# A mix stage rebuilt: entering states in their own slots, scans moved into the stage before, tiles backward, two buffers, a written-out pipeline

## What is computed

```
def step(S, blk):                      # one chunk of a scan
    ...
    o = A @ v + (q * exp(b)) @ S       # inside the chunk, and from the entering state S
    S = exp(b_end) * S + (k * exp(b_end - b)).T @ v
...
x = x + g1 * (concat[y_hg, y_ssd, y_ret] @ w_out)
h = rms_norm(x) * (1 + sc2) + sh2      # and then the router and the experts
```

## Time and profile before

| | us |
|---|---|
| three timed runs, median (lowest to highest) | 3216.76 (3212.91 to 3219.59) |
| the profiled execution, its own time | 3213.58 |
| span of the profiled execution | 3211.7 |
| mix stage of layer 0, barrier 3 to barrier 4 | 786.8 to 1094.1 |
| mix stage of layer 1 | 2349.5 to 2654.6 |
| PE busy, share of the span | 84% |
| DVE, POOL and ACT busy | 41%, 22% and 20% |

### The profile page before, as it was taken

One profiled execution on the slowest core, in us unless ns is written; L12 is line 12 of the kernel. 1 busy time (PEld: TensorE's weight loads), 2 busy tenths in 40 slices (PEclk: granted clock), 3 DMA queues, 4 the chain that ended last, 5 costly groups with the idle time before them and its releaser, 6 DMA issues.

```text
span 3211.7 us, 43754 instructions
## 1 busy us (share of the span) xinstructions
PE 2698.0 (84%) x16228; PEld 1980.1 (62%) x16228; DVE 1322.8 (41%) x2786; ACT 643.3 (20%) x1363; POOL 692.4 (22%) x782
## 2 busy tenths in 40 slices
PE   2899889998489569999769997999938982999992
PEld 0455566664255269999725555666525542999992
DVE  1355535555555432222105554455654545222221
ACT  0333312222011012211113332222211110122211
POOL 0000023443433112222100000444453320212211
PEclk9999989999688779999979998999968885999996
DMA  7432231112333447777373332211133324887763
GB/s 271 165 111 94 91 116 68 68 61 86 115 122 120 177 136 277 276 276 279 109 277 113 100 119 97 73 68 72 59 122 113 126 86 172 280 277 275 278 202 132
DMA packets 221546, 486.30 MB, mean 151 GB/s; under 512 B 26446, under 2 KB 82462, under 8 KB 218910
## 3 DMA queue, kind: packets, MB, share of 16 engines
q1 hardware_dynamic: 210046, 442.17, 38.3%
q0 software_dynamic: 11264, 37.76, 4.6%
q10 hardware_dynamic: 112, 4.72, 0.4%
HBM read 400.96 MB, written 88.36 MB: 152 GB/s over the span
## 4 chain that ended last, share of the span: by engine, by line
PE 73%; DVE 10%; DMA 5%; ACT 3%; issue 3%; POOL 2%; SPq 2%; POOLq 1%; DVEq 0%; ACTq 0%
PE bank L749 21%; PE bank L782 16%; PE bank L793 8%; PE bank L756 6%; DVE work L1404 6%; PE bank L720 5%; PE bank L839 4%; ACT work L1123 3%; PE bank L931 3%; DMA work<-gates_d 2%; PE bank L869 2%; PE bank L818 1%; DMA work<-x_d 1%; POOL small L1877 1%; PE bank L1047 1%
## 5 line engine op out<-in xcount | busy, mean ns | idle before, releaser
L749 PE MATMUL bank<-work 128*128 128x512 f32 (+1 forms) x1728 | 728.9, 569 | 13.3 <-ACT work L1123 8.7
L1123 ACT ACTIVATE work<-bank 128x256 f32<-128x256 f32 (+7 forms) x782 | 301.3, 419 | 1195.7 <-PE bank L782 256.9
L749 PEld LDWEIGHTS bank<-work 128*128 128x128 f32 x1728 | 316.3, 191 | 326.4 <-issue 287.2
L782 PE MATMUL bank<-work 128*128 128x144 f32 x4096 | 512.5, 288 | 2.2 <-DVE work L1404 2.2
L782 PEld LDWEIGHTS bank<-work 128*128 128x128 f32 x4096 | 508.8, 192 | 3.0 <-issue 2.4
L720 PE MATMUL bank<-cst,work 128*128 128x128 f32 (+3 forms) x1920 | 258.5, 284 | 217.1 <-DVE work L1839 87.9
L1404 DVE TENSOR_TENSOR work<-work 128x256 f32<-128x256 f32 (+3 forms) x629 | 356.3, 595 | 182.9 <-PE bank L931 98.7
L720 PEld LDWEIGHTS bank<-cst,work 128*128 128x128 f32 (+3 forms) x1920 | 220.8, 145 | 273.2 <-DVE work L1839 88.8
L1123 ACT ACTIVATE work<-work 128x256 f32<-128x256 f32 (+3 forms) x247 | 169.0, 685 | 980.0 <-DVE work L1404 376.3
L1404 DVE TENSOR_TENSOR work<-bank,work 128x144 f32<-128x144 f32 (+2 forms) x218 | 91.3, 421 | 544.4 <-ACT work L1123 503.3
L839 PE MATMUL bank<-work 128*128 128x512 f32 x576 | 273.2, 631 | 17.0 <-ACT work L1123 17.0
(11 more groups left out here) (155 smaller groups left out, 2343.8 us busy)
## 6 DMA issues: line engine op xcount, KB each, us to landing
work<-in_w_gate_dram SPq DMA_DIRECT2D x32, 2048.0 KB
work<-in_w_up_dram SPq DMA_DIRECT2D x32, 2048.0 KB
work<-in_w_down_dram SPq DMA_DIRECT2D x32, 2048.0 KB
work<-in_w_ada_dram SPq DMA_DIRECT2D x32, 1024.0 KB, 6.3
work<-x_d SPq DMA_DIRECT2D x45, 512.0 KB, 4.0
work<-sum_d SPq DMA_DIRECT2D x18, 1024.0 KB, 5.0
work<-in_w_ada_dram SPq DMA_DIRECT2D x4, 4096.0 KB, 19.2
work<-in_w_in_dram SPq DMA_DIRECT2D x8, 2048.0 KB, 19.6
```

The costliest lines, as they stand in the source:

```text
L749: mm = pe.matmul(bank[:, bk, 0:w.shape[-1]], h[:, ch, :], w[:, ch, :], start=(ch == 0), stop=(ch == DC - 1))
L782: mm = pe.matmul(bank[:, 4 + f, o:o + CAP_S + CAP_P], w[:, ch, f * P:(f + 1) * P], e_xt[:, ch, :], start=(ch == 0), stop=(ch == DC - 1))
L1123: return act.activation(out, in_, func, **kw)
```

## The change

Six things change, in all three stages of a layer that lie before the top-k choice.

1. **Slots.** The context's additions to the forward state go to slot 9 (`slot_f(0) = NT`), so the latents' entering states can be loaded at the start of the local stage (`load_states`) and the context's final states be stored inside it (`store_states`, behind tile 2). Tile 0 of the mix stage no longer multiplies with its zero states.
2. **Scans.** The forward scan is spread over the tiles of the local stage on POOL (`step_on`, one step behind `weighted_values` of tiles 2 to 8). The backward scan is done on POOL in the mix stage, two steps in the prologue and one per tile (`step_back`). The copies of `entering` are gone: `inter` reads the slots.
3. **Order.** The mix stage takes the tiles as 0, 8, 7, ..., 1 (`MIX`).
4. **Buffers.** `r_o`, `r_qe` and `r_g` have two sets; they, the gains, `w_out` and `r_x` lie over the weights of the stages before. ACT issues the load of `w_out` behind the last but one tile of the local stage, and SP the loads of tile 0 and of the gains there.
5. **Pipeline.** `mix` is split into `mix_states` and `mix_gate`, the loops are written out, and `inter` runs two tiles ahead of `project`; in a round PE does `turn_y(j)`, `inter(j + 2)`, `project(j, 0)`, `turn_xn(j - 1)`, `project(j, 1)`, `router(j - 1)`.
6. **State matmuls.** L967, L1038 and L1055 are split by head or group: twice the instructions, half the columns of weights and of moving data, each half written to its own 64 partitions. The copies out of the banks take 128 partitions at a time, half as many.

```diff
+        MIX = (0,) + tuple(range(NT - 1, 0, -1))
...
+        def slot_f(t):
+
+            return NT if t == 0 else (t + 1) % NT
...
+            def load_mix(l, j):
+                t, p = MIX[j], j % 2
+                if j >= 2:
+                    sp.wait_ge(sem["r_y"], by("r_y", l * NT + j - 1))
+                    sp.sem_inc(tick, 1)
+                name, _ = set_of(l, j)
+                sp.dma_start(r_o2[p], o_d[tile_rows(t), :]).then_inc(sem[name], 16)
+                sp.dma_start(r_g2[p], gates_d[tile_rows(t), :]).then_inc(sem[name], 16)
+                sp.dma_start(r_qe2[p].rearrange("p a b -> p (a b)"), qe_d[t]).then_inc(sem[name], 16)
...
                 load_sums(0, l * NT + 1)
+                load_states(l)
                 store_gates(0, l * NT + 1)
...
+                    if t == 2:
+                        store_states(l, l * NT + 1)
                     if t + 1 < NT:
                         store_gates(t + 1, n + 1)
+                    if t + 2 == NT:
+                        sp.wait_ge(sem["z_mm"], by("z_mm", n + 1))
+                        sp.sem_inc(tick, 1)
+                        load_mix(l, 0)
+                        load_res(0, l * NT + 1)
+                        for dst, src, m in ((gain_row[:, 0:256], hg_norm_g[l], 256), (gain_row[:, 256:768], ssd_norm_g[l], 512),
+                                            (gain_row[:, 768:1024], ret_norm_g[l], 256)):
+                            sp.dma_start(dst, row_bc(src, m)).then_inc(sem["gain_in"], 16)
                 for name in ("z_st", "l_st"):
                     sp.wait_ge(sem[name], by(name, l * NT + NT))
                     sp.sem_inc(tick, 1)
                 barrier(sp, l, 3)
...
+                load_mix(l, 1)
+                load_mix(l, 2)
+                load_mix(l, 3)
+                for j in range(1, NT):
+                    n = l * NT + j + 1
+                    load_res(MIX[j], n)
+                    store_sum(MIX[j - 1], n - 1)
+                    if j + 3 < NT:
+                        load_mix(l, j + 3)
+                    store_normed(MIX[j - 1], n - 1)
...
                     for i in range(4):
-                        mm = pe.matmul(bank[:, 2, i * P:(i + 1) * P], l_rkb[:, i * P:(i + 1) * P], l_rv[:, (i % 2) * P:(i % 2 + 1) * P], start=True, stop=True)
+                        for half in range(2):
+                            mm = pe.matmul(bank[rows(half), 2, i * HD:(i + 1) * HD], l_rkb[:, i * P + half * HD:][:, :HD], l_rv[:, (i % 2) * P + half * HD:][:, :HD],
+                                           start=True, stop=True)
...
                     for d in range(2):
-                        pe.matmul(bank[:, 6 + d, :], l_tm[:, 4, :], l_v2[:, d, :], start=True, stop=True).then_inc(sem["l_dS"], 1)
+                        for g in range(2):
+                            mm = pe.matmul(bank[rows(g), 6 + d, 0:256], l_tm[:, 4, g * HD:(g + 1) * HD], l_v2[:, d, g * 256:(g + 1) * 256], start=True, stop=True)
+                        mm.then_inc(sem["l_dS"], 1)
...
+                inter(l, 1)
+                pe.wait_ge(sem["a_rowcp"], by("a_rowcp", nl))
+                turn_y(l * NT + 1)
+                inter(l, 2)
                 pe.wait_ge(sem["r_w_in"], by("r_w_in", nl))
...
+                for j in range(1, NT):
+                    n = l * NT + j + 1
                     turn_y(n)
+                    if j + 2 < NT:
+                        if j >= 2:
+                            pe.wait_ge(sem["r_lgc"], by("r_lgc", n - 2))
+                        inter(l, j + 2)
                     project(n, 0)
                     turn_xn(n - 1)
                     project(n, 1)
...
+                    if t + 2 == NT:
+                        act.dma_start(r_w, w_out[l].rearrange("(c p) n -> p c n", p=P)).then_inc(sem["r_w_in"], 16)
...
-                for g in range(2):
-                    src = bank[rows(g), 2, :].rearrange("p (d q v) -> p d q v", d=2, q=2)[:, :, :, 64 * g:64 * g + 64]
-                    ev(st_f[rows(g), t + 1, RB[0]:RB[0] + 2, :], src[:, 0])
-                    last = ev(st_b[rows(g), t, RB[1]:RB[1] + 2, :], src[:, 1])
+                src = bank[:, 2, 0:256].rearrange("p (d q v) -> p d q v", d=2, q=2)
+                ev(st_f[:, slot_f(t), RB[0]:RB[0] + 2, :], src[:, 0])
+                last = ev(st_b[:, t, RB[1]:RB[1] + 2, :], src[:, 1])
...
-                ln = Link(dve, "s_fs", nl)
-                for tile in range(1, NT - 1):
-                    step_f = r_y[:, 0:512].rearrange("p (a b) -> p a b", b=HD)
-                    ln(tt(step_f, st_f[:, tile], bc(dec[:, tile, 0, :], HD)))
-                    ln(tt(st_f[:, tile + 1], st_f[:, tile + 1], step_f, ALU.add), last=(tile == NT - 2))
...
+                mix_gate(l, 0)
                 diagonal(0, nl)
                 diagonal(1, nl)
...
+                normed(l, 0)
+                spread(24, 8, scale2, shift2)
+                for j in range(1, 3):
+                    mix_states(l, j)
+                    mix_gate(l, j)
+                    sums(l * NT + j + 1)
+                    if j == 1:
+                        normed(l, 1)
...
+                for j in range(1, NT):
+                    n = l * NT + j + 1
+                    gated(0 if j == 1 else 1, n - 1)
+                    if j + 1 < NT:
+                        normed(l, j + 1)
+                    if j + 2 < NT:
+                        mix_states(l, j + 2)
                     second_norm(n - 1)
+                    if j + 2 < NT:
+                        mix_gate(l, j + 2)
+                    modulated(MIX[j - 1], n - 1)
+                    if j + 2 < NT:
+                        sums(n + 2)
+                    logits(MIX[j - 1], n - 1)
...
+            def step_back(l, t):
...
+                tt(r_step, st_b[:, t + 2], bc(dec[:, t + 1, 1, :], HD)).then_inc(sem["s_b"], 1)
...
+                tt(st_b[:, t + 1], st_b[:, t + 1], r_step, ALU.add).then_inc(sem["s_b"], 1)
...
+                pool.wait_ge(sem["l_incA"], by("l_incA", n))
+                pool.wait_ge(sem["l_incD"], by("l_incD", n))
+                pool.wait_ge(sem["l_rope"], by("l_rope", n + 1))
...
                     weighted_values(t, n)
+                    if t >= 2:
+                        step_on(l, t - 1)
                     if t + 1 < NT:
                         step_weights(t + 1, n + 1)
...
+                for j in range(1, NT):
+                    n = l * NT + j + 1
+                    residual(n - 1)
+                    if j + 2 < NT:
+                        gates(l, j + 2)
+                    if NT - 3 - j >= 1:
+                        step_back(l, NT - 3 - j)
+                    if j + 2 < NT:
+                        variances(n + 2)
```

More of the change, by code:

```diff
@@ L292, in trunk @@
         r_w = take(DC, D)
-        take = carve(S_END)
[L294 to L298, removed]
+        gain_row = take(D)
+        r_o2 = [take(D) for _ in range(2)]
+        r_g2 = [take(D) for _ in range(2)]
+        r_qe2 = [take(9, P) for _ in range(2)]
+        r_x = take(D)
+        take = carve(S_END)
         r_gg = take(D)
-        r_x = take(D)
         r_t = take(2, 512)
@@ L364, in __init__, with __call__ @@
                 self.eng, self.name, self.n, self.i = eng, name, n, 0
[L366 to L368 removed]
+            def __call__(self, ins, last=False, steps=1):
+                self.i += steps
+                ins.then_inc(sem[self.name], steps)
                 if last:
@@ L966, in _ @@
                     for i in range(4):
-                        mm = pe.matmul(bank[:, 2, i * P:(i + 1) * P], h_kb[:, i * P:(i + 1) * P], x[:, H_V + (i % 2) * P:][:, :P], start=True, stop=True)
+                        for half in range(2):
+                            mm = pe.matmul(bank[rows(half), 2, i * HD:(i + 1) * HD], h_kb[:, i * P + half * HD:][:, :HD], x[:, H_V + (i % 2) * P + half * HD:][:, :HD],
+                                           start=True, stop=True)
                     mm.then_inc(sem["h_dS"], 1)
@@ L1593, in tile_l @@
                     dve.sem_inc(tick, 1)
-                    for g in range(2):
-                        last = dve.tensor_copy((st_f[:, t + 1] if d == 0 else st_b[:, t])[rows(g), SB[d]:SB[d] + 4, :],
-                                               bank[rows(g), 6 + d, 256 * g:256 * g + 256].rearrange("p (a b) -> p a b", a=4))
-                    last.then_inc(sem["l_incD"], 1)
+                    dve.tensor_copy((st_f[:, slot_f(t)] if d == 0 else st_b[:, t])[:, SB[d]:SB[d] + 4, :],
+                                    bank[:, 6 + d, 0:256].rearrange("p (a b) -> p a b", a=4)).then_inc(sem["l_incD"], 1)
             def modulate_d(n):
```

250 lines of the change are left out of this document (107 added, 143 removed).

## The result

The changed kernel takes 3054.75 us (three runs, 3052.44 to 3058.83) against 3216.76: a ratio of 0.950, with a 95% interval of 0.948 to 0.952. The forecast was 3054.

A forecast was written before the change was run, and what follows sets the result against it. PE bound the local stage; a ring of waits of about 26 us per tile bound the mix loop. Prologue -46.7 - 43.7, loop -37.9 - 38.6, local end +8, tail +4.4, split -5: -159.5 from 3213.6, so 3054, range 3020 to 3098.

The forecast's parts named there:

- its DVE chain: Mix prologue: tile 0's gate to norm, second tile's states and gating, third tile's entering states, projection; 42.0 us, bounds 36 and 50.
- about 3 us are left, which a stall of DVE could use up: Mix loop: second norm is due 13 us into the round, behind some 10 us of other DVE work.
- rival 1: Mix loop: DVE and POOL block each other, +3 us in each of ten rounds, 3084 us; chance 0.15.
- I don't expect the faster level throughout: Mix loop: PE's clock still dips, taken as 1.25 of 3.0 us, so a round is 22.0 instead of 20.75.
- no wait over 1 us: Mix loop, new profile: PE's largest wait in a round should be under 1 us and never on a load.
- the late barrier: End of local stage: last store shares DMA engines with w_out, delaying barrier 3 by 4 us per layer, bounds 0 and 10.
- -2.5 for the split: State matmuls: zero for the narrow ones, -0.3 us for the SSD one in each of 16 tiles, -5 in all.
- rival 3: State matmuls: mode changes cost PE 3.0 us or more in each of 54 groups, 3215 us and above; chance 0.03.
- the +0.8: Narrow state matmuls: worst cost of the split in us each, against -0.55 at best; taken as zero.
- My limit of 8 us for the cover: Local stage: POOL's forward steps, 3.2 us per tile, cost nothing until they pass 8 us, hidden by POOL's waits for DVE.
- Rival 2: Mix loop: the load again ends the round, tiles stay at 25.5 us, only the prologue gains, 3131 us; chance 0.07.
- The tail: End of mix stage: router and its copy stand ahead of the last gating, +2.2 us per layer, 4.4 in all.

The follow-up runs named there:

- the reordered kernel: The changed kernel with DVE's loop list reordered, entering states of tile j+2 and second norm of tile j-1 ahead of the norm of tile j+1: 3040.36 us, ratio 0.946.
- the next version: The changed kernel with w_out issued behind barrier 3 and, in DVE's loop list, the second norm ahead of the next norm: 3022.55 us, ratio 0.940.

## Why the prediction came out right

**The prologue** was sized by its DVE chain, and the mechanism held: 42.0 forecast, 42.3 and 46.1 measured. In layer 0 the third tile's entering states start 22.4 us behind the barrier (22.0 forecast), take 5.5 (4.1), and the projection takes 14.5 (15.9). In layer 1 they start 24.8 us behind it and the projection takes 15.9, at a lower granted clock (0.74 instead of 0.82). Other kernels with the same prologue have both lengths in either layer: 43.3 and 43.2 with the new order of the loop, 46.0 and 45.9 without the split; DVE is busy for some 2 us more in the long ones. So 42.3 is at the lower end of a swing that I had not priced.

The scan put back costs some 20 us a layer, so taking it off this path is a large part of the gain. No edit puts the rest back, some 22 to 26 us a layer; for it stands this row of DVE's timeline before, 20 us behind barrier 3, the start of the old scan:

```profile
806.69 0.69 DVE L1404 TENSOR_TENSOR work<-work,dec 128x512 f32<-128x512 f32 x1 [16.63 <-DMA work<-in_state_ssd_dram]
```

The changed kernel loads these states in the stage before. What the order of the tiles and the dropped copies of `entering` are worth by themselves, no run shows.

**The loop** has the right length for a wrong reason. I put PE's list at 20.75 us and added 1.25 for dips of the clock. In this execution there are none: 1.00 throughout, and every half projection at 7.03 or 7.13 us. (The loop of layer 0 with the new order has one of 8.73.) PE's list is 20.3, as the reordered kernel shows, and up to 1.7 us a round were a wait for the second norm. It was in the prediction as "about 3 us are left, which a stall of DVE could use up", and as rival 1: DVE and POOL slow each other. The step that failed is "I don't expect the faster level throughout"; rival 1's mechanism held at a smaller size, 1.5 us a round over PE's list where the rival had 25 - 20.75 = 4.25. The forecast's own sign for this, no wait over 1 us, failed at 1.7.

**The end of the local stage** hid two errors that cancel. I took +4 for the late barrier and -2.5 for the split in each layer. Moving `w_out` gives back 7.2 us a layer, inside the bounds 0 and 10 but well over my 4; I let the store's bytes "go in turns" with `w_out` without pricing that for a store that all engines wait for. Nor was SP's 1.9 us a wait of the barrier before: SP was done at 786.0, and the barrier waited for DVE's drain behind its last copies. From the chain of the kernel before:

```profile
786.20 0.50 DVEq L356
```

And the split saves 5.0 a layer: I had zero for the narrow matmuls, which took 0.69 instead of 1.11 and so lie near my lower bound of -0.55 each. My rival 3, a price for each change of mode, does not show in these rows: the tiles are 0.41 us shorter. The Trainium skill's "TensorEngine Tiling (Array Packing)", "Tiling Modes", states that a change of mode drains the engine, without a price. Under "Performance Considerations" it states that a matmul of one column takes as long as one of 60. The narrow ones here have 64, so the +0.8 that I put down to the page was my own reading and not its figure.

**The scans** cost nothing where they went, as forecast. My limit of 8 us for the cover was not confirmed: steps of 9.8 us were still free in tiles 2 to 6, and where that cover ends no run shows. In tile 7 there is next to none.

**The buffers** are what the loop stands on. Rival 2 (the load stays last) had 3131; in the one form of a late load that was run, held for the norm of the tile before, it is 3276.

**The tail** was right, +2.4 and +2.3.

That the total was met within 1 us is luck: the terms are off by up to 4 us in both directions.

## What to carry to other kernels

A large transfer that is started early is not free if a small store that a barrier waits for is still to be issued: here it gained 14 us to put it behind the barrier, since its consumer left the time. Where one engine has become the bound, look at the order of its suppliers' lists: what it wants next stands first, and an instruction that works only in SBUF is kept away from the other engine's long ones. When a forecast comes out right, take its terms apart all the same: here two errors of some 3 us a layer cancelled each other, and a wait stood where a dip of the clock had been expected. The late barrier and that wait were worth some 14 us each to the next version.

## What the runs showed of the hardware

- DVE's 1,024-wide multiply takes 1.22 us by itself and 3.25 beside POOL's residual add, which takes 3.13 instead of 2.35. Instructions of DVE that read a bank were not slowed beside it (two of 256 columns: 0.42 and 0.41 us, and 0.41 each without it). The Trainium skill ("SBUF — State Buffer", "Who interferes with whom") states an exclusive lock on ports that the two engines share. The trace agrees: the ends of 859.18 and 860.26 are nearly those of taking turns.
- A 384 KB store took 10.58 us beside a 4 MB load and about 2.9 without it.
- Products of 64 columns written to two halves of the partitions overlap: sixteen records took 0.69 us where eight of 128 columns took 1.11, and where sixteen of 64 columns on the full width took 1.89.
- With gaps of 0.7 to 1.7 us in seven of eight rounds PE's granted clock stayed at 1.00 for 164 us.
